# Two-stage block on one core: token tiles kept apart at the stage borders, four split buffers and three raw ones, and weight units moved between stages

## What is computed

```python
h = h + mamba2_mixer(rms_norm(h, g_pre[0]), ...)
h = h + mla_mixer(rms_norm(h, g_pre[1]), k_nope, k_rope, v, ...)
x = layer_norm(rms_norm(h, g_final), ...)
# per layer: x = layer_norm(ALPHA * x + w_o(attention, fourier)); x = layer_norm(ALPHA * x + ffn(x))
```

## Time and profile before

| | |
|---|---|
| median of 3 runs | 1064.04 us |
| the profiled execution, its own time | 1063.66 us |
| its span, first to last instruction | 1061.9 us |
| mean granted TensorE clock | 0.987 |
| PE / PEld busy | 989.2 / 802.0 us |
| DVE / ACT / POOL busy | 526.9 / 475.3 / 521.5 us |
| instructions | 13606 |
| weights loaded by SP's queue | 142.62 MB in all |

### The profile page before, as it was taken

How to read it: one execution, slowest core, us unless ns; L and a number is a source line. 1 busy time by engine, 2 the same in 40 slices (tenths; PEclk the granted TensorE clock), 3 DMA queues, 4 the chain that set the end, 5 groups by cost and what they waited for, 6 DMA issues and landing times.

```text
span 1061.9 us, 13606 instructions
## 1 busy us (share of the span) xinstructions
PE 989.2 (93%) x5100; PEld 802.0 (76%) x5100; DVE 526.9 (50%) x903; ACT 475.3 (45%) x747; POOL 521.5 (49%) x240
## 2 busy tenths in 40 slices
PE   8989899898988998998989999998998989999995
PEld 6979677686867975876767888886977757888884
DVE  4697765744346647375442232236275552222324
ACT  5655644544446732474324344333375323343440
POOL 5243752573633033652445665665552544656652
PEclk9999999999989999999999999999999999999998
DMA  9444221354443024422343555554422225545520
GB/s 371 183 159 159 106 94 41 119 195 153 168 138 140 2 99 156 181 81 80 119 142 136 198 189 198 173 194 158 165 108 85 83 92 182 189 168 198 191 87 40
DMA packets 21803, 151.77 MB, mean 143 GB/s; under 512 B 2544, under 2 KB 2928, under 8 KB 3824
## 3 DMA queue, kind: packets, MB, share of 16 engines
q1 hardware_dynamic: 19872, 142.62, 38.1%
q10 hardware_dynamic: 1872, 8.34, 2.1%
HBM read 149.90 MB, written 1.05 MB: 142 GB/s over the span
## 4 chain that ended last, share of the span: by engine, by line
PE 75%; DVE 13%; ACT 6%; issue 3%; POOL 2%; DMA 1%; SPq 0%; POOLq 0%; DVEq 0%; ACTq 0%
PE ps L464 16%; PE ps L470 15%; PE ps L466 15%; PE ps L946 3%; PE ps L488 2%; PE ps L492 2%; PE ps L490 2%; ACT whi L1097 2%; PE ps L508 2%; DVE wlo L1485 1%; PE ps L618 1%; PE ps L963 1%; DVE res L1885 1%; DVE small L1874 1%; DVE arena L1882 1%
## 5 line engine op out<-in xcount | busy, mean ns | idle before, releaser
L2038 POOL TENSOR_TENSOR wlo<-raw,whi 128x1024 fp32r<-128x1024 f32 x134 | 427.0, 3189 | 427.7 <-ACT whi L1097 427.7
L1097 ACT CAST whi<-raw 128x2048 fp32r<-128x2048 f32 x134 | 255.9, 1912 | 194.3 <-PE ps L470 169.7
L1485 DVE TENSOR_TENSOR wlo<-raw,whi 128x1024 fp32r<-128x1024 f32 x134 | 183.8, 1372 | 292.1 <-ACT whi L1097 291.7
L464 PE MATMUL ps<-whi,ahi 128*128 128x512 f32 (+1 forms) x432 | 168.6, 390 | 8.8 <-DVE arena L2014 7.8
L466 PE MATMUL ps<-wlo,ahi 128*128 128x512 f32 (+1 forms) x432 | 168.0, 389 | 0.0
L470 PE MATMUL ps<-whi,alo 128*128 128x512 f32 (+1 forms) x432 | 162.8, 389 | 0.0
L464 PE MATMUL ps<-whi,bhi 128*128 128x512 f32 (+1 forms) x322 | 128.7, 400 | 6.7 <-issue 3.6
L466 PE MATMUL ps<-wlo,bhi 128*128 128x512 f32 (+1 forms) x322 | 125.1, 388 | 0.0
L464 PEld LDWEIGHTS ps<-whi,ahi 128*128 128x128 f32 x432 | 81.5, 189 | 27.2 <-DVE arena L2014 9.1
L470 PE MATMUL ps<-whi,blo 128*128 128x512 f32 (+1 forms) x322 | 101.7, 389 | 0.0
L470 PEld LDWEIGHTS ps<-whi,alo 128*128 128x128 f32 x432 | 81.5, 189 | 16.5
(11 more groups left out here) (261 smaller groups left out, 1586.4 us busy)
## 6 DMA issues: line engine op xcount, KB each, us to landing
raw<-in_wstream SPq DMA_DIRECT2D x134, 1024.0 KB, 4.8
par<-in_params ACTq DMA_DIRECT2D x5, 1024.0 KB, 5.1
tab<-in_tables ACTq DMA_DIRECT2D x1, 1352.0 KB, 8.6
res<-in_x SPq DMA_DIRECT2D x2, 512.0 KB, 4.4
out<-res SPq DMA_DIRECT2D x2, 512.0 KB, 2.6
wfs<-in_wf ACTq DMA_DIRECT2D x1, 512.0 KB, 11.3
par<-in_params ACTq DMA_DIRECT2D x1, 512.0 KB, 12.8
arena<-in_wsmall ACTq DMA_DIRECT2D x1, 256.0 KB, 8.6
```

The source lines that it names most:

```text
L464: pe.matmul(banks[t][b][:, 0:cw], h_, wh[:, i, c], start=st, stop=False, skip_group_check=True)
L1097: act.copy(whi[:, u % SPL, :], raw[:, u % RAW, :]).then_inc(w_hi, 1)
L1485: dve.tensor_tensor(wlo[:, u % SPL, c], raw[:, u % RAW, c], whi[:, u % SPL, c].bitcast(F32), ALU.subtract).then_inc(w_lo_v, 1)
L2038: pool.tensor_tensor(wlo[:, u % SPL, c], raw[:, u % RAW, c], whi[:, u % SPL, c].bitcast(F32), ALU.subtract).then_inc(w_lo_p, 1)
```

## The change

It has these parts, all at once.

1. **Buffers**: `RAW` 4 to 3, `SPL` 3 to 4, `AHEAD` 2 to 3. To make room, `wfs` moves into the arena and is loaded once a layer by ACT's queue, and `small` shrinks.
2. **Ends of stages**: `acc_units` takes `skew`; the last `skew` units run all for tile 0 and then all for tile 1: 4 for `mla_out`, 2 for `w_o`, still 1 for `ssm_out`. The last three `down` units do the same, and the last hidden tile's transpose stands inside them, directly ahead of the unit that needs it.
3. **Starts of stages**: `lead_units` in place of `first_pair`: the next four units (`vu` 0 to 3, or `gu` 0 and 1 with two units each) run for tile 0, with the transposes of tile 1 ahead of the fourth, and then for tile 1. The norms of DVE and POOL are ordered tile by tile, with single splits set between them. `u` is thus made ahead of the attention loop.
4. **Block attention**: `side_piece`s are only `qk` 1 and 3 (32 pieces, all by loop step 1); the Fourier steps stand at steps 3 to 8 and none after the last `diff_pv`; `o_banks` still waits for both tiles' `do_ss`.
5. **MLA**: `uq` 1, `kv_up` 1, `uq` 2, `gate` 2 and 3 are cut in 36 pieces of three matmuls, 6 ahead of the 16-head loop and 30 in its steps 0 to 6. The SiLU of the second gate half moves behind the loop.
6. **Mamba**: two z pieces a pair in place of three, and the last four half units (z 6, 7) after the loop; the dt series, the trigonometric part and the cumulative sums are spread over more steps (`CUM_AT` 6 to 7).
7. **Fillers**: `keep_busy` 5 to 2 ahead of the first y transposes, 4 to 0 in the MLA loop, (10, 4) to 2 and (2, 3) to 2 ahead of and behind the first tile's transposes at the start of each layer, 3 to 2 at the feed-forward's start.

```diff
-RAW, SPL = 4, 3
-AHEAD = 2
-DT_AT, CUM_AT, CB_AT = 1, 6, 9
+RAW, SPL = 3, 4
+AHEAD = 3
+DT_AT, CUM_AT, CB_AT = 1, 7, 9
...
+A_PIECES = {-1: 6, 0: 10, 1: 14, 2: 17, 3: 20, 4: 25, 5: 30, 6: 36}
...
 def fourier_steps(h):
-    return {6: [("pq", 0), ("f", 0)], 7: [("pq", 1), ("fy", 0), ("f", 1)],
-            8: [("pq", 2), ("fy", 1), ("f", 2)],
-            9: [("pq", 3), ("fy", 2), ("f", 3), ("fy", 3)]}.get(h, [])
+    return {3: [("pq", 0)], 4: [("f", 0), ("pq", 1)], 5: [("fy", 0), ("f", 1), ("pq", 2)],
+            6: [("fy", 1), ("f", 2), ("pq", 3)], 7: [("fy", 2), ("f", 3)], 8: [("fy", 3)]}.get(h, [])
...
-                for n in range(3 * p, 3 * p + 3):
-                    if n > 3 * p:
-                        scan_head(2 * p + n - 3 * p - 1)
-                    z_piece(4 + n // 4, n % 4)
+                z_piece(4 + p // 2, 2 * (p % 2))
+                scan_head(2 * p)
+                scan_head(2 * p + 1)
+                z_piece(4 + p // 2, 2 * (p % 2) + 1)
+            for q in range(12, 16):
+                z_half(q)
...
-            def acc_units(names, ah_of, first_wait):
+            def acc_units(names, ah_of, first_wait, skew=1):
...
+                for t in range(T):
+                    for n in range(whole, len(names)):
+                        name, kts, ready = names[n]
+                        if t == 0:
+                            ready()
+                        ah, al = ah_of(n)
+                        mm = tile_products(name, t, ah, al, kts, 2, D, banks[t], n == 0,
+                                           n == len(names) - 1)
+                        if t == T - 1:
+                            mm.then_inc(w_used, 1)
+                    if t == 0:
+                        mm.then_inc(acc_t0, 1)
...
+            def lead_units(names, fills, banks, acc):
...
                 for t in range(T):
                     wait_emptied(pe, FILL[(*fills, t, 1)])
+                    pe.wait_ge(acc_read, T * acc + t + 1)
                     for i, name in enumerate(names):
...
+                        if t == 0 and i == 3:
+                            turn_tile_when(fills, 1)
+                        mm = tile_products(name, t, ahi, alo, range(4 * (i % 2), 4 * (i % 2) + 4), 4, 512,
+                                           [banks[i // 2][t]], i % 2 == 0, i % 2 == 1)
...
# ACT, start of a layer
-                split.until(("vu", l, 0))
-                tile_hi(("h", l))
+                split.until(("vu", l, 2), 0)
+                tile_hi(("h", l), 0)
+                split.until(("vu", l, 3), 0)
+                tile_hi(("h", l), 1)
...
+                for t in range(T):
+                    if t == 0:
+                        act.wait_ge(lead_t0, 2 * l + 1)
+                    else:
+                        made(act, ("vu", l, 3))
+                    act.copy(u2[:, t, :], G[t]).then_inc(u_done, 1)
...
                 split.until(("qk", l, 0))
                 qk_out(0)
...
# PE, ends of the feed-forward and of a layer's attention
+                for t in range(T):
+                    for d in range(FF_UNITS - 3, FF_UNITS):
+                        name, kts = down(d)
+                        if t == 0:
+                            last_ready(d)()
+                        mm = tile_products(name, t, bhi, blo, kts, 2, D, [G[t], G[2 + t]], False,
+                                           d == FF_UNITS - 1)
...
                 def o_banks():
-                    pe.wait_ge(u_done, T * (l + 1))
+                    pe.wait_ge(qk_done, 4 * (l + 1))
                     pe.wait_ge(do_ss, T * (l + 1))
```

More of the change, by code:

```diff
@@ L474, in streamed @@
+                return mm
+            def streamed(name, ah, al, kts, nks, width, banks, first, last):
+                for t in range(T):
+                    mm = tile_products(name, t, ah, al, kts, nks, width, banks[t], first, last)
                 mm.then_inc(w_used, 1)
@@ L835, in mla_pv @@
                 mm.then_inc(o_psum, 1)
-            pe.wait_ge(q_rope, T)
+            for n in range(A_PIECES[-1]):
+                part(n)
             pe.wait_ge(k_rope, T)
@@ L1116, in _, with squares @@
             squared = [0]
-            def squares(n, src, width, wait=None):
+            def squares(n, src, width, wait=None, between=None):
                 if n:
@@ L1333, in _ @@
-            for c in range(3):
-                split.until(("uq", c))
-                made(act, ("uq", c))
-                b = (0, 2, 0)[c]
-                for t in range(T):
-                    ins = act.copy(qb[:, t, c * 512:(c + 1) * 512], G[b + t])
-                ins.then_inc(mc_read, 1)
+            split.until(("gate", 1))
+            act.wait_ge(sq_done, T * squared[0])
+            for t in range(T):
+                act.activation(gb[:, t, 0:512], X[t], ACT.Silu).then_inc(gate_done, 1)
@@ L1341, in mla_qk, with uq_out @@
+            def uq_out(c, t, bank):
+                act.copy(qb[:, t, c * 512:(c + 1) * 512], bank).then_inc(uq_read, 1)
+            split.until(("kv_up", 0))
+            made(act, ("kv_up", 0))
+            for c in range(2):
+                for t in range(T):
+                    kv_out(c, t, G[2 * c + t])
+            made(act, ("uq", 0))
+            for t in range(T):
+                uq_out(0, t, X[t])
+            split.until(("uq", 0))
             def mla_qk(h):
@@ L1357, in _ @@
             mla_qk(1)
+            for t in range(T):
+                part_ready(("uq", 1), t, 1)
+                uq_out(1, t, G[2 + t])
             mla_exp(0)
@@ L1389, in _ @@
                 qk_out(2)
-                split.until(("qk", l, 1))
                 def probs(n):
@@ L1794, in _ @@
                 link(rotate(kr[:, :, 0:HR], kr[:, :, HR:ROPE], t, 1))
-            for u in range(2):
-                split.until(("kv_up", u))
+            split.until(("kv_up", 0))
             for t in range(T):
@@ L1865, in _ @@
                     split.until(("mla_out", 0))
-            split.until(("mla_out", 3))
-            for t in range(T):
-                add_acc(1, t, ("mla_out", 3), 1.0, res)
+            split.until(("mla_out", 3), 0)
             def moments(n, t):
```

629 lines of the change are left out of this document (361 added, 268 removed).

## The result

The change made the kernel slower by half a percent: 1068.33 us in the median of 13 runs against 1063.22 us, ratio 1.0045 with a 95% interval of 1.0031 to 1.0059. The forecast was 1039.6 us, with 0.05 on slower. One run of the 13 took 1131.55 us at a mean clock of 0.834; it and one such run of the Fourier experiment are left out of every ratio and every mean of the clock. The profiled execution took 1066.31 us, its span is 1064.5, 2.6 more than before.

The account below looks back on a forecast made before the run. The prediction took PE's own sequence as the bound, so only its waits and fillers could gain. Its terms summed to -24.4 us, 1039.3 from the profiled 1063.66; with 0.4 for the median it forecast 1039.6 us, range 1025 to 1055.

Parts of the forecast that it names:

- The clock: Whole kernel: six falls of PE's clock to the lower level in place of five, +1.7 us, bounds -7 and +7.
- the two new waits: Block attention, each layer: PE idle 4.4 us ahead of `qk` 0 and 4.3 us ahead of `w_o`, within a +16.0 us term.
- Rival (c): Missing fillers: borders and waits without full cover bring ten clock falls in place of six, +6.8 us, 1046.5 us; chance 0.08.
- Convolution: Convolution stage: PE's wait of 3.53 us for the dt chain on DVE shrinks, 0.3 us left; -3.9 us.
- Scan and MLA: Scan: one z piece less per pair, -3.5 us. MLA: other units cover PE's waits and filler goes, -6.5 us.
- Border to layer 0: Between `mla_out` and layer 0: first product 5.2 us after the last one, against 13.9; -9.7 us, bounds -11 and -5.
- Borders in and behind the feed-forward: Feed-forward starts, -11.6 us for two layers, with a 2.05 us wait staying; border to layer 1, -4.7 us.
- The end: After PE's last product: 13.0 us becomes 9.4; with the hidden tile's 1.45 us, -2.2 us.
- rival (d): Weight loads: three raw buffers too few if a landing takes 13 us, +51 us, 1091 us; chance 0.04.
- Rival (e): Borders gain nothing because splits on POOL hold the roots, about 1063 us; chance 0.02.
- The sign: Whole kernel: faster 0.94, same 0.01, slower 0.05.

Follow-up runs that it names:

- the Fourier experiment: The changed kernel with the Fourier steps spread over attention loop steps 2 to 8 in place of 3 to 8: 1069.08 us, ratio 1.0033.
- Their edits: Two runs of the changed kernel: cast of `qk` 0 ahead of the u copy, 1063.95 us; `w_o` released by the head norm's reading step, 1063.03 us.
- the `gu` 2 edit: The changed kernel with PE's wait ahead of `gu` 2 set on hidden tile 0 alone instead of tiles 0 and 1: 1057.51 us, ratio 0.9952.

## Why the prediction was wrong

**The clock** is the step that failed: "Of five falls three go (65, 301, 311), one or two stay, and the two new waits of 4 us come in both layers: six for five, +1.7". The profile after has thirteen, 20.5 us more than before at full length. Three things were wrong in it. I counted only the waits that I had named, and left the smaller ones (2.6, 2.8, 3.1 us) without a fall though the trace of before had falls behind 1.7, 1.9 and 2.4. I took each fall at 1.7 us, while four were of twice the length. And the fillers that go were costed at nothing: with the new counts alone the kernel before has 15.5 us more deficit, with falls at 338 us, where the four calls of the MLA loop are gone, and ahead of layer 0, where eight are. Rival (c) was this mechanism; its ten falls were nearer to the thirteen, but it had 6.8 us and a chance of 0.08. What was measured directly is that filler alone gives 10.9 us back. From the slopes of 0.62 and 0.69 us for 1 us of deficit I estimate that the 20.6 us of added deficit cost 13 to 14 us of the time; at full length it would be 20. This estimate carries a slope over from one place to another, and the slopes differ: 0.16 and 0.3 in the old order, 0.4 without filler, the full length in the feed-forward. The rest of the 28.7 us by which the forecast missed, 10 to 17, is mis-sized waits.

The Trainium skill (TensorE: Matmul & The Clock Gate, A second HAM failure mode: psum-queue depth-cycling) says of another kernel that short idle pauses between groups of matmuls, frequent enough, make the clock go back and forth. The fall at 340 us, behind 0.99 and 1.10 us, agrees with that; the prediction weighed Part 1 alone. The Fourier experiment shows something else: behind a single wait of 2.7 us the clock stayed at 0.51 over 14 us in which PE was busy for 13.84.

**Convolution**, -3.9 forecast, -2.1 measured: "The use moves one unit (5.7 us) back". It did, and the last part of DVE's chain moved with it, behind the convolution of unit 6:

```profile
65.64 2.42 DVE L1727 SCALAR_TENSOR_TENSOR arena<-ps,vec,arena 128x255 f32<-128x255 f32 x6
67.98 0.87 DVE L1707 SCALAR_TENSOR_TENSOR small<-small 128x64 f32<-128x64 f32 x3
...
69.62 0.29 DVE L1713 TENSOR_TENSOR small<-small 128x32 f32<-128x32 f32 x2
```

PE waited 3.05 us for the row at 69.62, for 3.53 before. I had looked at where the consumer stands, not at where the producer went.

**Scan and MLA**: -3.5 and -6.5 forecast, -5.3 (with the output projection) and -7.1 measured, both inside their bounds. MLA had 0.8 us left ahead of the first scores in my sum and shows 2.99, as I read it because one of the small rotations took 2.28 us, its neighbours 0.23, with POOL in a split (last row, from its own timeline):

```profile
292.92 0.23 DVE L1916 TENSOR_TENSOR arena<-arena,trig 128x80 f32<-128x80 f32 x1
293.19 2.28 DVE L1917 TENSOR_TENSOR arena<-arena 128x80 f32<-128x80 f32 x1
295.40 0.23 DVE L1918 TENSOR_TENSOR arena<-arena 128x80 f32<-128x80 f32 x1
...
293.01 2.36 POOL L2197 TENSOR_TENSOR wlo<-raw,whi 128x1024 fp32r<-128x1024 f32 x1 [3.82 <-ACT whi L1166]
```

**Border to layer 0**: first product 5.2 us after the last one in the forecast, 7.9 measured (386.20 to 394.11). The stretch that I allowed came (3.31 us where it was 3.05), and PE had its filler and transposes as forecast. What I missed stands in ACT's order: the squares of tile 1, which wait for DVE's add, come ahead of tile 0's high part.

```profile
391.05 1.06 ACT L1196 ACTIVATE arena<-res 128x1024 f32<-128x1024 f32 x1 [5.57 <-DVE res L1869]
...
392.10 1.05 ACT L1220 CAST ahi<-ps 128x512 fp32r<-128x512 f32 x2
```

The transposes were complete at 389.8, so the high part is 2.3 us late, and the run with tile 0 served first confirms it: 5.2 us there. **Borders in and behind the feed-forward**: the wait ahead of `gu` 2 was forecast to stay at 2.05 and is 3.06, because only the transposes stand on PE between `gu` 1 and `gu` 2, and ACT takes the high part of hidden tile 0 first, then the SiLU of hidden tile 1 (last row), for which `gu` 2 waits:

```profile
547.64 3.73 ACT L1166 CAST whi<-raw 128x2048 fp32r<-128x2048 f32 x2
552.42 0.59 ACT L1207 CAST bhi<-ps 128x512 fp32r<-128x512 f32 x1 [1.06 <-PE ps L514]
552.90 0.67 ACT L1573 ACTIVATE arena<-ps 128x256 f32<-128x256 f32 x2
```

The first product of a feed-forward comes 7.5 us after the last one, not 6.6, and that of layer 1 7.0, not 6.0. **The end** was right: 9.35 us, 9.4 forecast.

**The two new waits** were right in place, cause and size: 3.8 and 4.3 us for 4.4 and 4.3, the first on a DVE split. Their edits confirm the causes. The stretch to `w_o` is 1.5 us longer in layer 1 than forecast and 0.2 shorter in layer 0, with the falls taken out at full length. **Buffers**, rival (d): no sign of it. **Rival (e)**, a return to about 1063, was closest in time and had 0.02, but its reason was wrong: the borders did gain, and the time came back elsewhere.

The sign was given 0.94 on a net gain of 26 us of waits. I never asked what the time would be if each of the waits left had a fall of 1.7 to 3.4 us behind it, which is the sum that decides.

## What to carry to other kernels

Where PE is over 90% busy, list every wait of PE of about 1 us or more that will be left after a change, not only the new ones, and price each with and without a fall of the clock; one profile does not say which of them will have it, for the next execution can place the falls elsewhere; a filler that covers a wait belongs to the work and must not be removed with the reason that the wait is shorter. When a consumer is moved, look where its producer stands in its own engine's order. And look at each wait for what it really needs: one constant at `gu` 2 gave more than any of the moves.

## What the runs showed of the hardware

- Falls of the clock are not tied to one wait: they follow waits of 1.4 us, and two of 1 us close together, and when one wait is covered or removed part of them comes up at others (deficit 34.2 to 29.2 and 33.0 us). Covering five kinds at once took the deficit to 18.4.
- The same wait has a fall behind it in one execution and not in another: the one of 2.99 us ahead of MLA's turned queries has none in the changed kernel's profile and has one in all ten profiles of variants that leave it bare.
- Between runs of one and the same kernel (the cast of `qk` 0 moved) the spans differ by 10 us (1054.7 to 1064.7), and the clock goes with them (0.977 to 0.962).
- 1 us of clock deficit cost 0.6 to 0.7 us of time in the changed kernel on average, its full length in the feed-forward (the `gu` 2 edit), and less elsewhere: 11.5 us for 28 without filler, 2.4 for 15.5 in the kernel before.
- Small DVE operations of 0.2 us took 2.3 to 2.4 beside a POOL split, twice on a path that PE waited for. The Trainium skill (Trainium Architecture — The Big Picture, What this means for kernel authors) has the port pair that DVE and GpSimd share as an exclusive lock, not a split of bandwidth. An operation that is over only when the pass of the other engine ends, as these rows show (POOL 293.01 to 295.37 us, DVE 293.19 to 295.47), agrees with that. What a hold lasts was not measured by itself.

Open is what in PE's activity brings a fall; the runs show its price and that filler in the waits takes most falls away, not its rule.
